# The beginning of a two-block transformer kernel, reordered: tokens and weights first, mem in the second head group, small rows through ScalarE's queue, angles on GpSimd

## Chip, cores and metric

The kernel runs on one core of a Trainium2 chip. The metric is the time of one launch on the device, in microseconds; lower is better.

## What is computed

256 tokens of width 1024 go through a first block of two layers and then a second block of two layers. All tensors are fp32. Each layer of the first block reads one large product of the tokens with `w_in` and splits it over three branches: a gated state-space branch (SSD, in both directions), differential attention with rotated queries and keys, and cross attention to 256 `mem` tokens.

```python
cos, sin = _rope_tables(positions)               # angle = position * inv_freq
for layer in range(2):
    proj = einsum('bsd,de->bse', x, w_in[layer])
    z, xbc, dt_raw, dq, dk, dv, dg, cq, cg, gl = split(proj)
    # SSD branch
    xbc = silu(conv5(xbc) + conv_b)              # 5 taps along the tokens
    dt = softplus(dt_raw + dt_bias);  a = -exp(a_log)
    y = scan(xs*dt[0], dt[0]*a[0], B, C) + flip(scan of the flipped) + d_skip*xs
    y_ssd = rmsnorm(y * silu(z))
    q, k = rope(dq, cos, sin), rope(dk, cos, sin)
    ...                                          # differential attention
    mem_kv = einsum('bmd,de->bme', mem, w_mem_kv[layer])
    ...                                          # cross attention, gates, output, layer norm
```

## The kernel before

**Products in three passes.** Weights come by DMA in units of 128 x 2048 fp32 (two transfers of 512 KB) into three raw buffers (`raw` slots 0 and 1, and `raw_third`, which lies in `scratch`). A unit is two weight tiles. `split(Q, p)` rounds tile p on ScalarE to a short mantissa (`w_hi`, L1082) and then VectorE stores the rest (`w_lo`, L1583). Four tiles are kept, so tile p+4 can be split only when TensorE has finished tile p. `x` and `mem` are split in the same way. TensorE's `proj` then runs 8 x 3 matmuls for each tile of 128 output columns (L583 to L585).

**Before the first product.** SyncE (SP) issues the identity, the positions, five constant columns, mem (two transfers, into `scratch`), x (two transfers), weight unit 0, the small rows (`early_params`, seven transfers), unit 1, then 16 transfers in `late_params` (the 1032 KB of constants, the step weights `w_dt` of both layers, `params_in` and the late rows). Unit 2 waits for `mem_ready`, because its buffer `raw_third` overlaps `mem_tok`. TensorE runs products with zeros (`idle_products`, L665) between transposing mem into four PSUM banks and x into four others (L673). VectorE works out the rotation angles (L1592 to L1608), ScalarE takes their sine and cosine.

**Head groups.** The SSD branch goes over four groups g of eight heads in each layer, each with tiles k = 0 to 15. For the six convolution tiles j = 0 to 5, ScalarE copies the PSUM bank to `conv_in`, applies the first tap, and splits weight tile j+4; VectorE adds the four other taps (`conv`, L1806), does its half of the split of tile j+4, and finishes the activation of tile j-1 (L1811). Tiles 6 to 9 are z, tiles 10 to 15 gates. In group 0 there is also the step size: `dt_tiles` (48 small matmuls, L732 to L734), `dt_exponent` and `dt_softplus` on VectorE ending in `a_tok` (L1792), the sums over tokens by `cumulate` (L743 to L750), and ScalarE's copies of these. Then, in every group, `spread_rows` (L792), the decays on ScalarE, `weigh` on VectorE (L1852) and `head_pair` on TensorE (L805).

**Order.** Each engine runs its own program in the order written, and the engines meet at semaphores. TensorE goes through group 0 of layer 0 as tile 0 (`first_tile`), transposes of rows, tiles 1 and 2, a wait for `tabs_in`, `dt_tiles`, tiles 3 to 8.

Of the kernel before, what the change touches and what calls it, by code (L numbers as in the profile page):

```python
# [7 lines left out]
F32 = mybir.dt.float32  # L8
# [7 lines left out]
P = 128  # L16
# [68 lines left out]
WARM_MEM, WARM_X, WARM_W = 4, 4, 8  # L85
# [75 lines left out]
def build(nc, a):  # L161
    ctx = ExitStack()
    with ctx:
# [107 lines left out]
        cut = Cut(SCRATCH - 2 * D)  # L271
        mem_tok = cut(2, D)

# [7 lines left out]
        mem_banks = (ps[5], ps[6], ps[0], ps[1])  # L281
# [55 lines left out]
        w_dt_in = sem("w_dt_in")  # L337
# [36 lines left out]
        def _(sp):  # L374
# [10 lines left out]
            load(pos_in, pos_i, spread(a["positions"][0]))  # L385
            const_cols(K_INV, 5, pos_in)
            for src, dst, s in ((a["mem"][0], mem_tok, mem_in), (a["x"][0], x_tok, x_in)):
# [4 lines left out]
            def early_params():  # L392
                load(rows_in, rows_a[0:PA_ROWS, :, :], a["conv_w"].rearrange("l k (t p) -> (k t) l p", p=P))
                for at, src in ((PB_CONVB, a["conv_b"]), (PB_NORM, a["ssd_norm_w"]), (PB_LNG, a["ln_g"]),
                                (PB_LNB, a["ln_b"]), (PB_DNW, a["diff_norm_w"])):
                    n = src.shape[1] // P
                    load(rows_in, rows_b[at:at + n, :, :], src.rearrange("l (t p) -> t l p", p=P))
                load(rows_in, rows_b[PB_GATE:PB_GATE + 24, :, :], a["gate_b"].rearrange("l b (t p) -> (b t) l p", p=P))

            def late_params():  # L400
                const_cols(P, K_INV - P, tabs_in)
                const_cols(K_SUB, P, tabs_in)
                for l in range(DEPTH):
                    load(w_dt_in, w_dt[:, l, :, :], a["w_in"][l].rearrange("(k p) c -> p k c", p=P)[:, :, DT0:DT0 + 64])
                    if l == 0:
                        for dst, src in ((neg_a, a["a_log"]), (dt_bias, a["dt_bias"])):
                            load(params_in, dst.rearrange("p l n -> p (l n)"), spread(src.rearrange("l d h -> (l d h)")))
                        load(params_in, skip_all.rearrange("p l n -> p (l n)"), spread(a["d_skip"].rearrange("l h -> (l h)")))
                        load(params_in, lam_in.rearrange("p l n -> p (l n)"), spread(a["diff_lam"].rearrange("l a b -> (l a b)")))
# [28 lines left out]
            for l in range(DEPTH):  # L438
                L = l * L1_Q
                for g in range(GROUPS):  # L440
                    Q = L + g * 4 + A_Q
                    cols(Q, 0, l, "w_in", X0 + g * 512)
                    if l == g == 0:
                        early_params()
                    cols(Q, 1, l, "w_in", X0 + 256 + g * 512)
                    if l == g == 0:
                        late_params()
                    if g == 0:
                        if l == 0:
                            sp.wait_ge(S["mem_ready"], 4)  # L450
                        else:
                            sp.wait_ge(S["merged_ready"], l * 4)
                    halves(Q, 2, l, "w_in", B0 + g * P, C0 + g * P)
# [67 lines left out]
        def _(pool):  # L521
# [8 lines left out]
            pool.memset(idle, 0.0).then_inc(S["idle_ready"], 1)  # L530
            pool.wait_ge(params_in, 16 * 4)
# [25 lines left out]
        def _(pe):  # L557
# [147 lines left out]
            def first_tile():  # L705
# [12 lines left out]
                pe.wait_ge(S["xT_ready"], 2)  # L718
                pe.wait_ge(tabs_in, 32)

            tri_le, tri_ge = mu[:, 0:P], ml[:, P:2 * P]
            for l in range(DEPTH):
                L, LH = l * L1_Q, l * L1_H + SETUP_H

                def dt_tiles():
                    pe.wait_ge(S["dt_lo_ready"], l + 1)
# [25 lines left out]
                for g in range(GROUPS):  # L752
                    Q, T, G = L + g * 4 + A_Q, LH + g * 8 + A_H, l * GROUPS + g
                    if g == 0:
# [4 lines left out]
                        dt_tiles()  # L759
                    for k in range(3 if g == 0 else 0, 9):  # L760
                        if l == g == 0 and k == 3:
                            pe.wait_ge(S["rows_free"], 1)
                        proj(Q, T, k, k, x1, own=ps[5] if g == 0 and k == 3 else None)
                        if l == g == 0 and k == 5:
# [14 lines left out]
                    if g == 0:  # L779
                        for k in range(9, 9 + 1):  # L780
                            proj(Q, T, k, k, x1)
                        cumulate()
# [294 lines left out]
        def _(act):  # L1077
# [60 lines left out]
            for b in range(4):  # L1138
                act.wait_ge(S["mem_turned"], b + 1)
                copy(mem_hi[:, 2 * b:2 * b + 2, :], pair(mem_banks[b])).then_inc(S["mem_hi_ready"], 1)  # L1140
            act.wait_ge(S["angles_ready"], 1)
            fn(sinT[:, :], red[:, 0, :], ACT.Sin, scale=const[:, K_SIGN:K_SIGN + 1])
            fn(cosT[:, :], red[:, 1, :], ACT.Sin).then_inc(S["rope_ready"], 1)
# [18 lines left out]
            act.wait_ge(tabs_in, 32)  # L1162

            def dt_weights(l):
                act.wait_ge(w_dt_in, 16 * DEPTH)
# [26 lines left out]
            dt_weights(0)  # L1192
            for l in range(DEPTH):
                L, LH = l * L1_Q, l * L1_H + SETUP_H
                turned_layers = l + 1
                for g in range(GROUPS):
# [9 lines left out]
                    zeros = view(const, K_CAUS2, 6, 2)  # L1206
                    copy(conv_in[:, :, 0:2], zeros)
                    copy(conv_in[:, :, 2 + SEQ:4 + SEQ], zeros)
                    for j in range(6):
# [7 lines left out]
                        split(Q, j + 4)  # L1217
# [1006 lines left out]
```

## Time and profile before

| | |
|---|---|
| median of 3 runs | 2443.31 us (2442.24 to 2443.97) |
| profiled execution | 2443.01 us, its span 2441.1 us |
| TensorE matmul | busy 2391.5 us (98%) |
| VectorE | busy 1713.4 us (70%) |
| ScalarE | busy 1339.5 us (55%) |
| GpSimd | busy 90.2 us (4%) |
| mean granted TensorE clock | 0.994 of full speed |

Times inside the profile count from the start of the span. The two clock levels of TensorE, 1.2 and 2.4 GHz, show as 0.5 and 1.0 in the column PEclk. A busy TensorE is not TensorE at its peak: the ends of matmuls are modelled, so starts are the better measure.

### The profile page before, as it was taken

The numbers are of one execution on the slowest core, as the hardware profiler recorded it, in microseconds if no ns is written. First come the engines' busy times: TensorE is split into PE (matmuls) and PEld (weight loads), VectorE is DVE, ScalarE is ACT, GpSimd is POOL, SyncE is SP. The second block draws the span as 40 slices with busy tenths as digits, with TensorE's granted clock in tenths as the row PEclk, the third lists the DMA queues.
The fourth block names the chain that finished last, engine by engine and source line by source line (L and its number), as shares of the span: only waits on it lengthen the run. The fifth ranks groups of instructions, "written<-read, shape, count | busy, mean of one in ns | idle before, by whom it ended". The sixth has DMA issues, their size and how long they took to land.

```text
span 2441.1 us, 48177 instructions
## 1 busy us (share of the span) xinstructions
PE 2391.5 (98%) x18842; PEld 2289.4 (94%) x18842; DVE 1713.4 (70%) x2517; ACT 1339.5 (55%) x2355; POOL 90.2 (4%) x101
## 2 busy tenths in 40 slices
PE   9999999999999999999999999999999999999998
PEld 8898999999899999999999997899999999789998
DVE  7788777777888867786766575676566657667665
ACT  6788655644678855563444445554444444555443
POOL 0000000000100000000100010010001001001000
PEclk9999999999999999999999999999999999999999
DMA  7454555455354455545455553345545544434553
GB/s 216 131 159 126 165 164 161 154 170 189 108 153 139 137 156 160 169 155 181 145 181 174 169 160 106 121 144 178 170 147 179 178 163 152 123 124 142 189 181 113
DMA packets 401046, 380.19 MB, mean 156 GB/s; under 512 B 28223, under 2 KB 397037, under 8 KB 400765
## 3 DMA queue, kind: packets, MB, share of 16 engines
q1 hardware_dynamic: 397821, 373.87, 48.0%
q10 hardware_dynamic: 3072, 4.20, 0.7%
q8 instruction: 106, 1.74, 0.3%
q14 instruction: 47, 0.39, 0.1%
HBM read 372.77 MB, written 1.05 MB: 153 GB/s over the span
## 4 chain that ended last, share of the span: by engine, by line
PE 79%; DVE 12%; ACT 3%; DVEq 3%; issue 1%; SPq 1%; DMA 1%; ACTq 0%
PE ps L583 22%; PE ps L585 21%; PE ps L584 21%; DVE scratch L1806 3%; DVE w_lo L1583 3%; DVEq L1805 2%; PE ps L805 2%; PE ps L836 1%; PE ps L837 1%; PE ps L838 1%; ACT scratch L1082 1%; ACT w_hi L1082 1%; PE ps L854 1%; PE ps L612 1%; PE ps L614 1%
## 5 line engine op out<-in xcount | busy, mean ns | idle before, releaser
L1583 DVE TENSOR_TENSOR w_lo<-raw,w_hi 128x1024 fp32r<-128x1024 f32 x664 | 812.0, 1229 | 423.2 <-ACT w_hi L1082 421.8
L583 PE MATMUL ps<-x_hi,w_hi 128*128 128x256 f32 (+1 forms) x3664 | 1056.4, 288 | 4.3 <-DVE w_lo L1583 1.6
L584 PE MATMUL ps<-x_lo,w_hi 128*128 128x256 f32 (+1 forms) x3664 | 1042.6, 285 | 0.0
L585 PE MATMUL ps<-x_hi,w_lo 128*128 128x256 f32 (+1 forms) x3664 | 1039.8, 284 | 0.0
L1082 ACT ACTIVATE w_hi<-raw 128x1024 fp32r<-128x1024 f32 x664 | 697.7, 1056 | 447.5 <-PE ps L585 370.6
L583 PEld LDWEIGHTS ps<-x_hi,w_hi 128*128 128x128 f32 x3664 | 690.8, 189 | 30.8 <-issue 25.3
L584 PEld LDWEIGHTS ps<-x_lo,w_hi 128*128 128x128 f32 x3664 | 692.2, 189 | 2.0
L585 PEld LDWEIGHTS ps<-x_hi,w_lo 128*128 128x128 f32 x3664 | 693.6, 189 | 0.0
L583 PE MATMUL ps<-big_r,w_hi 128*128 128x272 f32 (+1 forms) x832 | 238.9, 287 | 0.0
L585 PE MATMUL ps<-big_r,w_lo 128*128 128x272 f32 (+1 forms) x832 | 238.2, 286 | 0.0
L1082 ACT ACTIVATE scratch<-ps 128x256 f32<-128x256 f32 (+9 forms) x328 | 122.3, 384 | 154.9 <-PE ps L838 63.8
L584 PE MATMUL ps<-gates_r,w_hi 128*128 128x272 f32 (+1 forms) x704 | 201.3, 286 | 0.0
L584 PE MATMUL ps<-big_r,w_hi 128*128 128x256 f32 (+1 forms) x640 | 181.3, 283 | 0.0
L1079 ACT ACTIVATE scratch<-ps 128x256 f32<-128x256 f32 (+2 forms) x168 | 66.6, 399 | 168.8 <-PE ps L585 153.8
L585 PEld LDWEIGHTS ps<-big_r,w_lo 128*128 128x128 f32 x832 | 156.6, 188 | 0.0
L583 PEld LDWEIGHTS ps<-big_r,w_hi 128*128 128x128 f32 x832 | 156.3, 188 | 0.2
L583 PE MATMUL ps<-scratch_r,w_hi 128*128 128x256 f32 x512 | 144.2, 282 | 2.6 <-DVE scratch L1995 2.6
L585 PE MATMUL ps<-scratch_r,w_lo 128*128 128x256 f32 x512 | 144.7, 283 | 0.0
L584 PEld LDWEIGHTS ps<-gates_r,w_hi 128*128 128x128 f32 x704 | 132.5, 188 | 0.1
L584 PEld LDWEIGHTS ps<-big_r,w_hi 128*128 128x128 f32 x640 | 120.1, 188 | 0.1
L527 POOL TENSOR_TENSOR xT<-xT,norm_bias 128x272 f32<-128x272 f32 (+1 forms) x56 | 52.0, 961 | 1688.4 <-DVE x_lo L1713 1688.4
L1806 DVE SCALAR_TENSOR_TENSOR scratch<-scratch,pa_all 128x256 f32<-128x256 f32 x192 | 93.5, 487 | 24.8 <-ACT scratch L1079 12.7
(302 smaller groups left out, 3063.1 us busy)
## 6 DMA issues: line engine op xcount, KB each, us to landing
raw<-in_w_in SPq DMA_DIRECT2D x184, 512.0 KB, 4.7
raw<-in_ffn_w_up SPq DMA_DIRECT2D x176, 512.0 KB, 4.3
raw<-in_ffn_w_down SPq DMA_DIRECT2D x64, 512.0 KB, 4.2
raw<-in_mix_w_in SPq DMA_DIRECT2D x64, 512.0 KB, 4.6
scratch<-in_w_in SPq DMA_DIRECT2D x40, 512.0 KB, 4.8
raw<-in_w_mem_kv SPq DMA_DIRECT2D x32, 512.0 KB, 4.8
raw<-in_w_br_ssd SPq DMA_DIRECT2D x32, 512.0 KB, 3.8
raw<-in_ffn_w_down SPq DMA_DIRECT2D x32, 384.0 KB, 3.3
```

The costliest lines, as they stand in the source:

```text
L527: m = pool.tensor_tensor(x, x, norm_bias[:, o:o + 1].to_broadcast([P, n]), ALU.add)
L583: mm(out, wh, xh, start=first, stop=False)
L584: mm(out, wh, xl, start=False, stop=False)
L585: return mm(out, wl, xh, start=False, stop=last)
L612: mm(out, w_hi[:, o, j, :], x[0][:, j, :], start=(j == 0), stop=False)
L614: mm(out, w_lo[:, o, j, :], x[0][:, j, :], start=False, stop=False)
L805: m = mm(b[e * 64:(e + 1) * 64, q], x_dt[:, 2 * d + t, j * 64:(j + 1) * 64], decay[:, j % 4, w], start=(n == 0), stop=(n == 3), skip_group ...
L1079: return act.activation(out, in_, f, **kw)
L1082: return act.activation(out, in_, ACT.Copy, scale=scale)
L1583: tt(w_lo[:, p % PARTS, :, :], raw_at(slot_of(Q, p))[:, :, (p % 2) * P:(p % 2 + 1) * P], wh_f[:, p % PARTS, :, :], ALU.subtract).then_inc( ...
L1805: v.drain()
L1806: m = stt(c, conv_in[:, j, n:n + SEQ], tap(n), c, ALU.mult, ALU.add)
```

## The change

- **SP's order:** identity, x, unit 0, unit 1, then `step_params` (positions, five constant columns, `w_dt` of layer 0, the four `params_in` transfers), unit 2 without a wait, then `late_params` (constants and late rows), units 3 and 4. After unit 4 SP waits for `rope_ready` and issues mem and `w_dt` of layer 1. mem_tok now lies in `gates`, over the angle buffers.
- **Small rows:** the seven transfers of `early_params` are issued by ScalarE as its first work.
- **Angles:** the work is moved from VectorE to GpSimd. A fused multiply-add becomes a `tensor_scalar` and a `tensor_tensor`: 15 instructions, most of them behind a drain.
- **Sine and cosine:** on ScalarE after `dt_weights(0)`, ahead of the first convolution tile, instead of ahead of x.
- **mem:** transposed, copied and split in group 1 of layer 0: `turn_mem(b)` stands before tile k = 2b on TensorE, `mem_copy(b)` on ScalarE behind the split of tile 2b+4 (the last one behind z tile 0), `mem_rest(b)` on VectorE behind the split of tile 2b+4 (the last one ahead of `conv_silu(5)`). One PSUM bank, ps[5], serves all four; from b = 1 on TensorE waits until `mem_rest(b-1)` is done.
- **dt_tiles** of layer 0 come after tile 4 instead of after tile 2; `dt_exponent` and its Exp two convolution tiles later. The waits for the constants move to just before their first use.

```diff
-WARM_MEM, WARM_X, WARM_W = 4, 4, 8
+WARM_X, WARM_W = 8, 8
...
+        mem_tok = view(gates, 4096, 2, D)
...
+            tokens_in(a["x"][0], x_tok, x_in)
...
+            def step_params():
+                load(pos_in, pos_i, spread(a["positions"][0]))
+                const_cols(K_INV, 5, pos_in)
+                step_weights(0)
...
                     cols(Q, 1, l, "w_in", X0 + 256 + g * 512)
                     if l == g == 0:
+                        step_params()
+                    if g == 0 and l:
+                        sp.wait_ge(S["merged_ready"], l * 4)
+                    halves(Q, 2, l, "w_in", B0 + g * P, C0 + g * P)
+                    if l == g == 0:
                         late_params()
-                    if g == 0:
-                        if l == 0:
-                            sp.wait_ge(S["mem_ready"], 4)
...
                     cols(Q, 4, l, "w_in", Z0 + 256 + g * 512)
+                    if l == g == 0:
+                        sp.wait_ge(S["rope_ready"], 1)
+                        tokens_in(a["mem"][0], mem_tok, mem_in)
+                        step_weights(1)
...
+            pool.wait_ge(pos_in, 32)
+            pool.tensor_copy(red[:, 2, :], pos_i)
+            pool.drain()
+            pts(an, red[:, 2, :], const[:, K_INV:K_INV + 1], None, ALU.mult)
...
+            for c in (C1, C2, C3):
+                pool.drain()
+                pts(red[:, 1, :], red[:, 3, :], -c, None, ALU.mult)
+                pool.drain()
+                ptt(an, red[:, 1, :], an, ALU.add)
...
+            pts(red[:, 1, :], red[:, 1, :], PI_DOWN, -PI_DOWN, ALU.min, ALU.max).then_inc(S["angles_ready"], 1)
             pool.wait_ge(params_in, 16 * 4)
...
             pe.wait_ge(S["idle_ready"], 1)
-            idle_products(ps[7], WARM_MEM)
+            idle_products(ps[7], WARM_X)
             pe.wait_ge(ident_in, 16)
-            turn_tokens(mem_tok, mem_banks, mem_in, "mem_turned")
-            idle_products(ps[7], WARM_X)
             turn_tokens(x_tok, x_banks, x_in, "x_turned")
-            pe.wait_ge(S["mem_ready"], 1)
             idle_products(ps[5], WARM_W)
-            pe.wait_ge(S["mem_ready"], 4)
+
+            def turn_mem(b):
+                pe.wait_ge(mem_in[b // 2], 16)
+                if b:
+                    pe.wait_ge(S["mem_ready"], b)
+                for f in range(2 * b, 2 * b + 2):
+                    for t in range(2):
+                        m = pe.transpose(ps[5][:, (f % 2) * SEQ + t * P:(f % 2) * SEQ + (t + 1) * P], mem_tok[:, t, f * P:(f + 1) * P], ident)
+                m.then_inc(S["mem_turned"], 1)
...
+                        if l == 0 and g == 1 and k in (0, 2, 4, 6):
+                            turn_mem(k // 2)
                         proj(Q, T, k, k, x1, own=ps[5] if g == 0 and k == 3 else None)
+                        if l == g == 0 and k == 4:
+                            dt_tiles()
...
             x_copy(0)
             x_copy(1)
             dt_weights(0)
+            rope_tables()
+            act.wait_ge(S["idle_ready"], 1)
...
                         split(Q, j + 4)
+                        if l == 0 and g == 1 and j in (0, 2, 4):
+                            mem_copy(j // 2)
...
                         split(Q, j + 4)
+                        if l == 0 and g == 1 and j in (0, 2, 4):
+                            mem_rest(j // 2)
                         if j:
                             conv_silu(j - 1)
-                        if g == 0 and j == 1:
+                        if g == 0 and j == (1 if l else 3):
                             dt_exponent()
```

## Rows read from the trace of the kernel before

**Rows 1.** Timeline, SyncE's queue: start us, us, queue line, transfer, count.
```profile
2.13 0.94 SPq L390 DMA_DIRECT2D scratch<-in_mem  x2
```

**Rows 2.** Timeline, first 32 us: start us, us, engine, instruction [idle before, releaser].
```profile
7.54 3.17 PE L673 MATMUL ps<-const,scratch 128*128 128x128 f32 x16 [2.65 <-DMA scratch<-in_mem]
...
18.06 0.36 PE L710 MATMUL ps<-x_hi,w_hi 128*128 128x256 f32 x1
...
18.08 2.01 ACT L1082 ACTIVATE w_hi<-raw 128x1024 fp32r<-128x1024 f32 x2 [0.66 <-DMA raw<-in_w_in]
...
25.15 0.30 ACT L1082 ACTIVATE scratch<-const 128x12 f32<-128x12 f32 x2
...
30.25 1.06 ACT L1082 ACTIVATE w_hi<-scratch 128x1024 fp32r<-128x1024 f32 x1 [3.84 <-DMA scratch<-in_w_in]
```

**Rows 3.** Windows from the start: busy of PE, PEld, DVE, ACT, POOL; PEclk, DMA share, GB/s.
```profile
0.00:9.00 9.00, 5.24 (x17) 3.76 (x18) 2.85 (x9) 1.96 (x3) 0.52 (x5) 0.95 0.69 206
...
0.00:18.00 18.00, 14.24 (x64) 11.75 (x64) 9.94 (x21) 9.72 (x14) 0.52 (x5) 0.91 0.90 278
```

**Rows 4.** Timeline, VectorE, group 0: conv(0), w_lo of tile 4.
```profile
26.72 2.16 DVE L1806 SCALAR_TENSOR_TENSOR scratch<-scratch,pa_all 128x256 f32<-128x256 f32 x4
31.34 1.22 DVE L1583 TENSOR_TENSOR w_lo<-scratch,w_hi 128x1024 fp32r<-128x1024 f32 x1 [2.46 <-ACT w_hi L1082]
```

**Rows 5.** Timeline, TensorE, group 0: start of dt_tiles, of tile 3, of cumulate.
```profile
27.07 0.19 PE L732 MATMUL ps<-w_dt_hi,x_hi 128*128 128x64 f32 x1
...
32.61 0.56 PE L583 MATMUL ps<-x_hi,w_hi 128*128 128x256 f32 x1
...
57.98 0.30 PE L743 MATMUL ps<-a_tok,const 128*128 128x32 f32 x1 [1.23 <-DVE a_tok L1792]
```

**Rows 6.** Timeline, GpSimd: a fill, four copies with drains, two adds of one shape.
```profile
0.74 0.31 POOL L530 MEMSET gates<- 128x256 f32 x1 [0.29 <-POOLq L2212]
23.66 1.15 POOL L535 COPY skip<-skip_all 64x16 f32<-64x16 f32 x4 [22.61 <-DMA gates<-in_diff_lam]
...
90.40 1.47 POOL L549 TENSOR_TENSOR y_sum<-y_sum,y_sq 128x256 f32<-128x256 f32 x1 [8.50 <-ACT y_sq L1079]
95.03 0.74 POOL L549 TENSOR_TENSOR y_sum<-y_sum,y_sq 128x256 f32<-128x256 f32 x1 [3.17 <-ACT y_sq L1079]
```

**Rows 7.** Timeline, ScalarE: sine and its cosine before; a table load ahead of a wait.
```profile
12.66 0.51 ACT L1079 ACTIVATE sinT<-gates,const 128x256 f32<-128x256 f32 x1
...
319.39 1.28 ACT L1079 ACT_TABLE_LOAD   x1
324.69 0.63 ACT L1079 ACTIVATE scratch<-scratch 128x512 f32<-128x512 f32 x1 [4.02 <-DVE scratch L1968]
```

**Rows 8.** Windows, TensorE alone: us, busy (count), PEclk, DMA share, GB/s.
```profile
8.50:12.00 3.50, 3.50 (x15) 0.56 1.07 374
...
32.00:35.30 3.30, 3.30 (x17) 0.51 0.91 290
...
623.00:633.20 10.20, 10.20 (x50) 0.52 0.39 117
```

**Rows 9.** Timeline, TensorE, group 1: starts of tiles 1, 2, 8, and head pair 0.
```profile
95.03 0.28 PE L583 MATMUL ps<-x_hi,w_hi 128*128 128x256 f32 x1
...
97.88 0.28 PE L583 MATMUL ps<-x_hi,w_hi 128*128 128x256 f32 x1
...
115.34 0.36 PE L583 MATMUL ps<-x_hi,w_hi 128*128 128x256 f32 x1 [0.18 <-DVE w_lo L1583]
...
128.31 1.52 PE L805 MATMUL ps<-big,scratch 128*64 128x256 f32 x16 [1.11 <-DVE big L1852]
```

**Rows 10.** Timeline: ScalarE's copy of tile 0 in group 1, VectorE's split behind conv(0), mem's split.
```profile
96.61 0.36 ACT L1082 ACTIVATE scratch<-ps 128x256 f32<-128x256 f32 x1
...
100.14 1.22 DVE L1583 TENSOR_TENSOR w_lo<-raw,w_hi 128x1024 fp32r<-128x1024 f32 x1
...
9.94 2.48 DVE L1616 TENSOR_TENSOR mem_lo<-ps,mem_hi 128x512 fp32r<-128x512 f32 x4
```

More of the change, by code:

```diff
@@ L336, in build @@
         late_rows_in = sem("late_rows_in")
-        w_dt_in = sem("w_dt_in")
+        w_dt_in = [sem(f"w_dt_in{l}") for l in range(DEPTH)]
         rot_in = [sem("q_rotated_in"), sem("k_rotated_in")]
@@ L384, in _, with tokens_in @@
             const_cols(K_ID, P, ident_in)
-            load(pos_in, pos_i, spread(a["positions"][0]))
-            const_cols(K_INV, 5, pos_in)
-            for src, dst, s in ((a["mem"][0], mem_tok, mem_in), (a["x"][0], x_tok, x_in)):
+            def tokens_in(src, dst, s):
                 for h in range(2):
@@ L390, in _, with step_weights @@
                     sp.dma_start(dst[:, :, c], src.rearrange("(t p) d -> p t d", p=P)[:, :, c]).then_inc(s[h], 16)
[L392 to L398, printed above, removed]
+            tokens_in(a["x"][0], x_tok, x_in)
+            def step_weights(l):
+                load(w_dt_in[l], w_dt[:, l, :, :], a["w_in"][l].rearrange("(k p) c -> p k c", p=P)[:, :, DT0:DT0 + 64])
+            def step_params():
+                load(pos_in, pos_i, spread(a["positions"][0]))
+                const_cols(K_INV, 5, pos_in)
+                step_weights(0)
+                for dst, src in ((neg_a, a["a_log"]), (dt_bias, a["dt_bias"])):
+                    load(params_in, dst.rearrange("p l n -> p (l n)"), spread(src.rearrange("l d h -> (l d h)")))
+                load(params_in, skip_all.rearrange("p l n -> p (l n)"), spread(a["d_skip"].rearrange("l h -> (l h)")))
+                load(params_in, lam_in.rearrange("p l n -> p (l n)"), spread(a["diff_lam"].rearrange("l a b -> (l a b)")))
             def late_params():
@@ L781, in _ @@
                             proj(Q, T, k, k, x1)
+                        pe.wait_ge(tabs_in, 32)
                         cumulate()
@@ L1136, in pair, with load, mem_copy, rope_tables @@
                 return bank[:, :].rearrange("p (f s) -> p f s", f=2)
-            for b in range(4):
-                act.wait_ge(S["mem_turned"], b + 1)
[L1140 to L1143, printed above, removed]
+            def load(s, dst, src):
+                act.dma_start(dst, src).then_inc(s, 16)
+            load(rows_in, rows_a[0:PA_ROWS, :, :], a["conv_w"].rearrange("l k (t p) -> (k t) l p", p=P))
+            for at, src in ((PB_CONVB, a["conv_b"]), (PB_NORM, a["ssd_norm_w"]), (PB_LNG, a["ln_g"]),
+                            (PB_LNB, a["ln_b"]), (PB_DNW, a["diff_norm_w"])):
+                n = src.shape[1] // P
+                load(rows_in, rows_b[at:at + n, :, :], src.rearrange("l (t p) -> t l p", p=P))
+            load(rows_in, rows_b[PB_GATE:PB_GATE + 24, :, :], a["gate_b"].rearrange("l b (t p) -> (b t) l p", p=P))
+            def mem_copy(b):
+                act.wait_ge(S["mem_turned"], b + 1)
+                copy(mem_hi[:, 2 * b:2 * b + 2, :], pair(ps[5])).then_inc(S["mem_hi_ready"], 1)
+            def rope_tables():
+                act.wait_ge(S["angles_ready"], 1)
+                fn(sinT[:, :], red[:, 0, :], ACT.Sin, scale=const[:, K_SIGN:K_SIGN + 1])
+                fn(cosT[:, :], red[:, 1, :], ACT.Sin).then_inc(S["rope_ready"], 1)
             def x_first(b):
@@ L1203, in conv_tanh @@
                         fn(xbc_t[:, j % 2, :], xbc[:, j, :], ACT.Tanh).then_inc(S["conv_tanh"], 1)
-                    zeros = view(const, K_CAUS2, 6, 2)
+                    zeros = view(gates, 0, 6, 2) if l == g == 0 else view(const, K_CAUS2, 6, 2)
                     copy(conv_in[:, :, 0:2], zeros)
@@ L1226, in _ @@
                                 late_copies()
-                        if g == 0 and j == 2:
+                        if g == 0 and j == (2 if l else 4):
                             act.wait_ge(S["dt_pre"], l + 1)
@@ L1240, in _ @@
                     z_tile(0)
+                    if l == 0 and g == 1:
+                        mem_copy(3)
                     conv_tanh(5)
@@ L1589, in _, with mem_rest @@
             v.sem_inc(lo_ready, LO_CREDIT)
[L1590 to L1608 removed]
             def pair(bank):
                 return bank[:, :].rearrange("p (f s) -> p f s", f=2)
[L1613 removed]
+            def mem_rest(b):
                 v.wait_ge(S["mem_hi_ready"], b + 1)
                 t = slice(2 * b, 2 * b + 2)
[L1616 removed]
+                tt(mem_lo[:, t, :], pair(ps[5]), mem_hi[:, t, :].bitcast(F32), ALU.subtract).then_inc(S["mem_ready"], 1)
             def x_rest(b):
```

63 lines of the change are left out of this document (21 added, 42 removed).

## Prediction

> **What bounds the kernel now.** I read the busy shares first. TensorE is busy 98% of the span and at full clock nearly all the time, so over the whole launch there are only some 50 us that an edit of the order could win back, and the edit touches the first 130 us alone. I then read the timeline of the start. The first product begins at 18.06; before it mem is waited for, turned and split, and only then x [rows 2]. The chain that ended last runs through the first 31 us as SP issues, one transfer (unit 2), and ScalarE's split of tile 4: that split begins at 30.25 after 3.84 of waiting for the transfer [rows 2]. VectorE has finished conv(0) by then and starts the rest of tile 4 at 31.34 [rows 4]. From there VectorE has hardly a gap until `a_tok`, and TensorE waits 1.23 for it and starts the sums at 57.98 [rows 5]. So an earlier product at the start is worth nothing by itself: what counts is when tile 4 is split, and what engine is the last one at 57.98.
>
> In group 1 TensorE is the bound, but only just. It is delayed 0.18 before tile 8 and 1.11 before head pair 0 by VectorE [rows 9]. VectorE needs about 3.55 us for each convolution tile (2.15 for four taps, 1.15 for the split, 0.35 for the activation; rows 4 and 10 show the first two), TensorE 2.85 [rows 9]. TensorE gets through the nine tiles because it enters them with four tiles split ahead.
>
> **The start.** x is asked for at the place where mem was or earlier (mem at 2.13 [rows 1]), about 0.9 us sooner. Mem's first half ended TensorE's wait at 7.54 [rows 2], so x's should by about 6.4. ScalarE's seven issues fit before that, in a stretch where it only waited. The first product can then begin some 4 to 5 us earlier than 18.06, near 13.3. Tiles 0 to 3 and the rows take 11.8 us, so TensorE is through with tile 3 near 25.1 and then has nothing until tile 4 is split. I count no gain for this.
>
> Unit 1 before was waited for until 18.08, with 4.6 MB asked for up to it (identity, positions, mem, x, two units, rows). Between 9 and 18 us the queue moved (278 x 18 - 206 x 9) / 9 = 350 GB/s [rows 3]. Up to the positions and constant columns there are now 3.6 MB, 1.0 MB less or 2.9 us, and the stream starts 0.9 sooner: they land near 14.3. Unit 2 has 1.8 MB more before its end: near 19.5. It is no longer late. The mem transfers come behind unit 4 and the sines, and have 40 us before their use: nothing.
>
> **The angles now set tile 4.** ScalarE does the sines before the first convolution tile and in order, so the conv, the split of tile 4 and all that follows stand behind `angles_ready`. GpSimd runs 15 instructions: 11 with one input, 4 with two. The trace has no one-input arithmetic there; its bounds are the fill of the same shape, 0.31, and the add, 0.74 by itself and 1.47 beside a VectorE split [rows 6]. A drain adds 0.1: four tiny copies of which each takes 0.19 spread over 1.15. I take 0.4 for the one-input form, nearer the fill, since it too has one stream to move. Sum: 11 x 0.52 + 4 x 0.86 = 9.2, and 1.0 for meeting the last splits of tiles 2 and 3. Angles are ready at 14.3 + 10.2 = 24.5. With 0.31 and no meeting it is 22.5; with 0.92 for one input (twice my 0.4, and more) and 1.47 for the four adds, 32.
>
> The GPSIMD Engine Reference of the Trainium skill (Engine selection, Specifications) sends elementwise work to VectorE, calls two-input work about twice as slow on GpSimd and one-input work roughly line-rate, and says that two-input VectorE instructions contend with it. The trace agrees on the last: the same add took 0.74 and 1.47. By that page one-input work would be nearer the lower bound, and the sum would come out nearer 23.
>
> The sine's table load costs 1.28 but was made ahead of a wait elsewhere (load at 319.39, instruction at 324.69 [rows 7]); here it is hidden in the same way. Sine and cosine cost 0.9 [rows 7]: 25.4. From ScalarE's zeros at 25.15 to the end of conv(0) at 28.88 took 3.7 [rows 2, 4]; I take 3.5, without the wait in it for VectorE's other work. So conv(0) ends at 28.9 and VectorE splits tile 4 from 28.9 to 30.1, 2.4 us sooner than before.
>
> **The last engine of group 0.** VectorE needs 57.98 - 31.34 = 26.6 from there to `a_tok`: 55.5. TensorE before ran from tile 3 at 32.61 to 56.75 (57.98 less the wait of 1.23 [rows 5]), 24.1, of which 1.35 is the half clock until 35.3 [rows 8]. At full clock, less tile 3 (2.85) and with dt_tiles (27.07 to 32.61, 5.2 at full clock [rows 5]), it needs 22.8 - 2.85 + 5.2 = 25.2 from tile 4 on. dt_tiles used to fill the wait for unit 2; now they come behind it. So TensorE idles some 4.8 us, and is then the last engine: 30.1 + 25.2 = 55.3, plus the clock. After an idle stretch of 2.65 [rows 2] the granted clock fell to 0.56 (8.5 to 12), and behind dt_tiles to 0.51 (32.0 to 35.3) and in layer 1 for 10.2 us [rows 8]. One such stretch costs 1.7; here there are both causes, so 1.7 to 3.4. The sums begin between 57.0 and 58.7, against 57.98. I take -0.3 for group 0.
>
> **Mem in group 1.** TensorE now does 16 transposes, VectorE four splits of 0.62 [rows 10], ScalarE four copies of 0.6. Before, they lay ahead of the first product. The larger cost is the wait in `turn_mem(b)`. It asks that VectorE be through conv(2b-2) and the split of tile 2b+2, which TensorE needs only two tiles later. All in times of before, with copy, tap and conv 3.5 (96.61 to 100.14 [rows 10]):
> - Tile 0 starts 0.5 late, for its own transposes; tile 1 ends at 97.88 + 0.5 = 98.4. VectorE ends the split of tile 4 at 101.3 and mem's at 101.95. TensorE waits 3.5, transposes 0.5, and starts tile 2 at 102.5 instead of 97.88.
> - Tile 2 ends at 105.35; conv(2) and its split follow, 3.5 + 1.2, then mem's: 110.65. Tile 3 ended at 108.2. Wait 2.4; tile 4 at 111.1.
> - Tile 4 ends at 113.95; 117.5, 119.3. Tile 5 ended at 116.8. Wait 2.5; tile 6 at 119.8, tile 8 at 125.5 instead of 115.34.
>
> That is 10.2 late at tile 8. TensorE cannot give it back: it has no other gap than the 1.11 before head pair 0, which goes, because VectorE is now ahead. Net +9.1. An idle stretch of 3.5 is longer than the 2.65 after which the clock fell, so I add one half-clock stretch, +1.7. Behind that, queued on TensorE, the spread rows, head pairs and gate tiles of group 1 all shift; group 2 starts late by the same amount.
>
> The sum is 2443.0 (the profiled execution's own time, 0.3 under the median) - 0.3 + 9.1 + 1.7 = 2453.5, and as a median 2453.5 too within its error.
>
> **Rivals.**
> - *Fast angles (not slower by more than the bound).* If the positions land by 11 and the one-input form costs 0.31, the angles are ready by 19.5, unit 2 lands at the same time, and tile 4 is ready before TensorE ends tile 3 at 25.1. Then there is no idle stretch: 25.1 + 25.2 + 1.7 = 52.0, 6.0 sooner. With +9.1 in group 1 and no fall of the clock there, 2446. It decides once angles are ready before 21. For it: the fill's 0.31 and the short queue. Against it: 3.6 MB ahead of the positions at 350 GB/s.
> - *Slow angles.* At 32, tile 4 comes 7.5 later: 2461. For it: 1.47 beside splits; against it: the splits end by 17.
> - *The clock.* The 10.2 us of half clock in layer 1 [rows 8] cost 5.1; if that stretch is cut to 3.4 us by the shift in time, 3.4 come back: 2450. If both mem waits and dt_tiles bring a stretch more, 2456.
> - *Mem is covered after all (faster).* If TensorE's waits were as short as VectorE's added work, group 1 would cost 2.5; with the fast angles that gives 2443.0 - 6.0 + 2.5 = 2439.5, and with the shorter stretch of layer 1, 2436. Against it: the wait is written before tile 2, and VectorE cannot be done before 101.9.
>
> **Chances.** My forecast with its clock variants (2449 to 2457) 0.55, fast angles 0.22, slow angles 0.13, mem covered 0.10. The range reaches from between fast angles and no change to slow angles, 2444 to 2461. Within 0.2% is within 4.9 us, about what a measurement of this kernel can tell from no change. Slower: 0.55 + 0.13; within: 0.22 and a part of the last, 0.25; faster: 0.07.
>
> **What would show it.** In the profile after: the first product near 13.3; VectorE free of angles; 15 GpSimd instructions ending near 24.5 and the sine right behind; unit 2 not waited for; TensorE idle some 5 us before tile 4, then dt_tiles; `cumulate` near 57.7. In group 1, three waits of TensorE for VectorE's mem split before tiles 2, 4 and 6, of 3.5, 2.4 and 2.5, and no wait before head pair 0. The prediction is wrong if the angles come before 21 or after 28, if the waits in group 1 are under 1 us each, or if the stretches of half clock move by more than one.

## The result, and the profile after

The changed kernel takes 2464.75 us (median of 4, 2459.12 to 2465.14) against 2443.64 before: ratio 1.0083, interval 1.0071 to 1.0095. It is slower by 21 us, outside the range given and twice the 10 us forecast. The profiled execution took 2465.14 us, its span is 2463.3 us, 22.2 longer than before.

The tiles of TensorE show where the time went. The first two rows are the changed kernel's: first product and tile 4. The others are the starts of group 1 and group 2 (timeline, TensorE: start us, us).

```profile
14.31 0.36 PE L735 MATMUL ps<-x_hi,w_hi 128*128 128x256 f32 x1 [0.82 <-issue]
...
38.70 0.58 PE L603 MATMUL ps<-x_hi,w_hi 128*128 128x256 f32 x1 [12.37 <-ACT scratch L1111]
...
104.13 0.36 PE L603 MATMUL ps<-x_hi,w_hi 128*128 128x256 f32 x1
...
174.20 0.39 PE L603 MATMUL ps<-x_hi,w_hi 128*128 128x256 f32 x1
```

The same point, the start of group 2, in the kernel before (timeline, TensorE):

```profile
149.85 0.39 PE L583 MATMUL ps<-x_hi,w_hi 128*128 128x256 f32 x1
```

The first product is 3.7 us sooner than at 18.06 [rows 2], and that bought nothing. Tile 4 started at 36.81 before; now it is at 38.70, behind a gap of 12.37. Group 1 began at 92.08 before and now at 104.13: 12.05 us were lost in group 0 (0.4 of it is mem's first transposes, which stand just ahead of this mark). Group 2 is 24.35 late, so group 1 lost 12.3 more. After that 2.15 us come back, most of it in the half clock of layer 1 (6.8 us of it instead of the 10.2 of [rows 8]). "Half clock" here and below is a stretch in which the column PEclk shows 0.5.

**Group 0.** GpSimd in the changed kernel (timeline: start us, us, what ended the idle time):

```profile
15.68 0.40 POOL L530 CAST gates<-gates 128x256 f32<-128x256 int32 x1 [14.63 <-DMA const<-constants]
16.33 2.80 POOL L532 TENSOR_SCALAR gates<-gates,const 128x256 f32<-128x256 f32 x1 [0.25 <-issue]
19.29 0.41 POOL L534 TENSOR_SCALAR gates<-gates 128x256 f32<-128x256 f32 x1 [0.15 <-issue]
19.84 0.86 POOL L536 TENSOR_SCALAR gates<-gates 128x256 f32<-128x256 f32 x1 [0.15 <-issue]
20.86 0.97 POOL L539 TENSOR_SCALAR gates<-gates 128x256 f32<-128x256 f32 x1 [0.15 <-issue]
21.98 0.73 POOL L541 TENSOR_TENSOR gates<-gates 128x256 f32<-128x256 f32 x1
...
30.24 0.40 POOL L550 TENSOR_SCALAR gates<-gates 128x256 f32<-128x256 f32 x1 [0.16 <-issue]
```

GpSimd can start on the positions at 15.68, and its chain takes 15.0 us. The two-input adds cost 0.73, as the row of before had it [rows 6]. The one-input `tensor_scalar` instructions are of two kinds, 0.41 and 0.85 or more, and the first took 2.80. ScalarE waits for the end of it (timeline, ScalarE, changed kernel):

```profile
20.05 1.28 ACT L1108 ACT_TABLE_LOAD   x1
30.68 0.51 ACT L1108 ACTIVATE sinT<-gates,const 128x256 f32<-128x256 f32 x1 [9.34 <-POOL gates L550]
...
37.12 0.29 ACT L1108 ACTIVATE neg_a<-neg_a 128x128 f32<-128x128 f32 x1
37.44 0.71 ACT L1111 ACTIVATE head_sel<-const 64x32 fp32r<-64x32 f32 x3
38.17 0.20 ACT L1108 ACTIVATE stats<-stats 128x4 f32<-128x4 f32 x1
38.28 0.37 ACT L1111 ACTIVATE scratch<-ps 128x256 f32<-128x256 f32 x1
```

and VectorE has two splits beside the 2.80 of GpSimd, tile 4's split and, later, a wait (timeline, VectorE, changed kernel):

```profile
16.05 2.36 DVE L1630 TENSOR_TENSOR w_lo<-raw,w_hi 128x1024 fp32r<-128x1024 f32 x2 [0.71 <-ACT w_hi L1111]
...
34.76 1.22 DVE L1630 TENSOR_TENSOR w_lo<-scratch,w_hi 128x1024 fp32r<-128x1024 f32 x1
...
51.20 0.22 DVE L1787 TENSOR_TENSOR big<-ps,dt_bias_b 128x64 f32<-128x64 f32 x1 [3.90 <-PE ps L758]
```

The table load is indeed hidden in the wait. Tile 4 is split from 34.76 to 35.98, and yet TensorE starts it 2.7 us later: it waits for a count that ScalarE raises with its copy of tile 2 (38.28), which stands behind `small_params` (37.12 to 38.28). The count is stricter than the data: tile 4 goes into ps[0], whose tile 0 ScalarE copied at 31.60, and tile 2 lies in ps[6], but the copies of tiles 0 and 2 raise one semaphore, and `bank` asks for both:

```python
def bank(T, k):
    pe.wait_ge(gf[k % 2], T + k // 2 + 1)
...
bank = {2: ps[6], 3: ps[5]}.get(j, ps[j % 2]) if g == 0 else ps[j % 2]
copy(conv_in[:, j, 2:2 + SEQ], bank[:, 0:SEQ]).then_inc(gf[j % 2], 1)
```

Then VectorE waits 3.90 for `dt_tiles`. Part of TensorE's work here runs at half clock, as its windows of the changed kernel show (us, busy (count), PEclk, DMA share, GB/s):

```profile
31.00:44.60 13.60, 5.90 (x28) 0.50 0.60 191
48.00:54.80 6.80, 6.80 (x34) 0.50 0.43 146
75.40:82.20 6.80, 6.27 (x27) 0.50 0.00 0
```

The first stretch begins inside the gap, so only 5.9 us of it are work. The step-size sums begin at 69.69 instead of 57.98, and TensorE has no wait ahead of them, so it is the last engine, as forecast (timeline, TensorE, changed kernel):

```profile
69.69 1.42 PE L767 MATMUL ps<-a_tok,const 128*128 128x32 f32 x12
```

Between tile 3 and the sums the kernel before had one stretch, from 32.0 to 35.3 [rows 8]; now there are the first two. The third lies behind the start of the sums, where the kernel before had 6.8 us as well.

**Group 1.** TensorE's waits in the changed kernel over the whole span (who waited for whom: us in total, times, longest):

```profile
PE ps L603 <- ACT scratch L1111: 12.4, 1, 12.4
PE ps L709 <- DVE mem_lo L1643: 8.3, 3, 3.3
...
PE ps L834 <- DVE big L1882: 6.1, 6, 1.1
```

and two of the waits with mem's transposes and the tile behind the first (timeline, TensorE):

```profile
113.38 1.09 PE L709 MATMUL ps<-const,gates 128*128 128x128 f32 x4 [3.30 <-DVE mem_lo L1643]
114.12 0.56 PE L603 MATMUL ps<-x_hi,w_hi 128*128 128x256 f32 x1
...
133.74 1.09 PE L709 MATMUL ps<-const,gates 128*128 128x128 f32 x4 [2.62 <-DVE mem_lo L1643]
```

The third wait, of 2.33, ends at 123.36. Each comes with 3.4 us of half clock, which begins inside the wait (windows, changed kernel):

```profile
112.90:116.30 3.40, 2.92 (x14) 0.50 0.00 0
```

The two others begin near 123.2 and 133.5. The wait before head pair 0 [rows 9] is gone.

### The profile page after: what moved, and what is told of

Its sections match the earlier page's. It is cut to its first block, busy times and chain, and to the rows that moved or that the text cites. A ratio compares the mean times of both kernels' runs of the same rounds, so it can differ in the third digit from the quotient of the medians.

```text
span 2463.3 us, 48167 instructions
## 1 busy us (share of the span) xinstructions
PE 2397.1 (97%) x18842; PEld 2296.0 (93%) x18842; DVE 1711.4 (69%) x2506; ACT 1339.4 (54%) x2355; POOL 103.0 (4%) x116
## 4 chain that ended last, share of the span: by engine, by line
PE 80%; DVE 11%; ACT 4%; DVEq 2%; issue 2%; DMA 1%; POOLq 1%; ACTq 0%; SPq 0%; POOL 0%
PE ps L603 22%; PE ps L605 22%; PE ps L604 22%; DVE scratch L1831 3%; DVE w_lo L1630 2%; PE ps L834 2%; DVEq L1830 1%; PE ps L865 1%; PE ps L866 1%; PE ps L867 1%; ACT scratch L1111 1%; ACT w_hi L1111 1%; DMA raw<-in_ffn_w_up 1%; PE ps L883 1%; DVE xT L1732 1%
```

## The experiments

All are edits of the changed kernel unless a line says otherwise. Marks are from the profiled execution, one for each kernel, in us from its start. The launches are medians and were taken on different chips; the ratio is to the kernel before on the same chip, so launches are best compared by it.

| kernel | sine starts | tile 4 | group 1 | group 2 | launch | ratio (interval) |
|---|---|---|---|---|---|---|
| before | 12.66 | 36.81 | 92.08 | 149.85 | | 1 |
| changed | 30.68 | 38.70 | 104.13 | 174.20 | 2464.75 | 1.0083 (1.0071 to 1.0095) |
| a1 angles on VectorE | 24.94 | 32.97 | 98.20 | 170.21 | 2461.74 | 1.0070 (1.0054 to 1.0087) |
| a2 four banks | 30.00 | 38.02 | 103.48 | 162.88 | 2454.40 | 1.0043 (1.0027 to 1.0060) |
| a3 dt_tiles early | 30.78 | 38.81 | 98.13 | 168.12 | 2458.19 | 1.0062 (1.0045 to 1.0079) |
| a4 two-operation forms | 28.12 | 36.15 | 99.11 | 169.64 | 2462.41 | 1.0080 (1.0063 to 1.0096) |
| b1 = a1 + a2 + a3 | 25.69 | 34.24 | 91.03 | 150.78 | 2443.26 | 1.0002 (0.9993 to 1.0012) |
| b2 positions first | 21.16 | 29.21 | 93.57 | 163.64 | 2455.26 | 1.0048 (1.0032 to 1.0063) |
| b3 all mended | 20.91 | 34.24 | 87.22 | 146.99 | 2439.85 | 0.9984 (0.9975 to 0.9993) |
| b4 gap filled | 30.40 | 38.43 | 99.95 | 170.45 | 2466.02 | 1.0097 (1.0082 to 1.0113) |
| c1 copy freed | 29.73 | 36.59 | 95.97 | 166.53 | 2464.27 | 1.0087 (1.0071 to 1.0102) |
| c2 halves, both layers | 20.87 | 30.96 | 84.55 | 144.32 | 2439.91 | 0.9985 (0.9976 to 0.9994) |
| c3 filled and banks | 31.03 | 39.06 | 100.44 | 159.82 | 2454.67 | 1.0043 (1.0028 to 1.0059) |
| d1 halves, layer 0 | 21.47 | 31.56 | 85.14 | 144.92 | 2437.43 | 0.9978 (0.9969 to 0.9987) |

The intervals of a1, a3, a4, b4 and c1 overlap that of the changed kernel: for these the marks show where time moved, and a gain of the launch is not shown by itself. The marks also hold what half clock that one execution had. The clearest case is c1: its group 1 starts 8.2 sooner than in the changed kernel although tile 4 is only 2.1 sooner, since this execution had 10.2 us of half clock ahead of group 1 instead of 27.2.

### Angles back on VectorE

```diff
-            pool.wait_ge(pos_in, 32)
...
             dt_weights(0)
             lam_products()
+            v.wait_ge(pos_in, 32)
+            v.tensor_copy(red[:, 2, :], pos_i)
...
```

> The changed kernel with the twelve angle instructions back on VectorE, behind its work on the step weights and lambda. In the changed kernel GpSimd had the angles ready at 30.64 us and ScalarE had waited 9.34 us for them. If the GpSimd chain is what sets tile 4 (theory), VectorE starts at about 21.6, needs 4.4 us as before, sine follows at 26.0, and everything behind it moves up by 4.6 us; TensorE's gap of 12.4 us before tile 4 shrinks to about 7.8, and with less half clock the launch gains 4.6 to 8 us. If the place of the sines in ScalarE's order or its copy of tile 2 is what counts and not the engine (rival), the launch moves by less than 1.5 us.

The sine starts 5.7 us sooner (4.6 expected), tile 4 also 5.7. The gap is 7.98 and the half clock that begins in it 10.2 us instead of 13.6. Some 1.4 of the 5.7 is the first product, which came sooner in this execution. Group 2 is only 4.0 sooner, with 3.4 us more of half clock in group 1 (6.8, 3.4 and 3.4), and the launch 3.0, under the 4.6 expected and within the intervals. GpSimd's chain is on the path to tile 4; what it costs the launch this run alone does not show.

### Four banks for mem

```diff
                 pe.wait_ge(mem_in[b // 2], 16)
-                if b:
-                    pe.wait_ge(S["mem_ready"], b)
...
-                copy(mem_hi[:, 2 * b:2 * b + 2, :], pair(ps[5]))
+                copy(mem_hi[:, 2 * b:2 * b + 2, :], pair(mem_banks[b]))
```

`mem_banks` holds ps[5], ps[7], ps[2] and ps[3], and the split of the low part reads the same bank.

> The changed kernel with four PSUM banks for mem (ps[5], ps[7], ps[2], ps[3]) instead of one, so that TensorE no longer waits for VectorE's split of the last pair; mem's work and places stay. If the single bank's handshake is the cost in group 1 (theory), the three waits of 3.30, 2.33 and 2.62 us go, TensorE then keeps VectorE's pace and reaches tile 8 about 7 us sooner, the three half-clock stretches (3.4 us each, 1.7 us of loss each) go too: 8 to 13 us in all. If mem's own work on VectorE and ScalarE is the cost and the waits only show it (rival), the time comes back before tile 8 or head pair 0 and the launch gains under 3 us.

From group 1 to group 2 it takes 59.4 us, against 70.1 in the changed kernel and 57.8 before. The three waits and the three stretches of half clock are gone; two small waits for VectorE are back in their old places (0.94 where it was 0.16 before, and 1.10 before head pair 0). The launch gains 10.4, and its interval is clear of the changed kernel's. Mem's own work in group 1 costs 1.6, besides the 0.4 of transposes ahead of the mark; the single bank's handshake costs 10.7. Nearly all of the 10.7 can be named: 8.25 of waits and 4.1 of clock (each of tiles 2, 4 and 6 takes 3.9 to 4.0 us instead of 2.9, and the transposes ahead of it 0.74 instead of 0.41), less the two small waits that come back.

### dt_tiles early

```diff
                             first_three(Q, T, x1, l * KT, SEQ)
-                            dt_tiles()
+                        dt_tiles()
...
-                        if l == g == 0 and k == 4:
-                            dt_tiles()
```

> The changed kernel with dt_tiles back behind tile 2, so that they fill the gap of 12.4 us before tile 4. If their place cost time (theory), TensorE loses their 7 us at half clock behind tile 4, VectorE's waits for them (0.46 and 3.90 us) go, and the launch gains 7 to 12 us. If group 0 is set by VectorE's chain from the split of tile 4 to a_tok anyway (rival), it gains only VectorE's waits, 4 us or less.

Tile 4 stays where it was (38.81, gap 4.04) and tile 5 starts at 43.09 instead of 50.98. Group 1 is 6.0 sooner and the launch 6.6. TensorE now waits 1.40 for `a_tok`: VectorE's chain is the next bound, so the gain is under the 7 us expected but above the rival's 4.

### Two-operation forms on GpSimd

```diff
+            pts(an, idle, 1.0, 0.0, ALU.mult, ALU.add)
             pool.wait_ge(pos_in, 32)
...
-                pts(red[:, 1, :], red[:, 3, :], -c, None, ALU.mult)
+                pts(red[:, 1, :], red[:, 3, :], -c, 0.0, ALU.mult, ALU.add)
```

> The changed kernel with the five tensor_scalar instructions of GpSimd that have one operation (0.85 to 0.97 us each) given a second one that changes nothing (times 1 or plus 0), and a tensor_scalar on zeros while GpSimd waits for the positions. If the one-operation form is the slow one (theory), each falls to the 0.41 of the two-operation forms, 2.3 us together. If the 2.80 us of the first tensor_scalar were the first use of the form, it falls to below 1; if they are its per-partition scalar, it stays at 2.8. The angles come 2.3 to 4.3 us sooner and the launch gains that, up to 2 us more with the clock. Rival: the times go with the operations and values and not with the form: the five stay at 0.85 or more, no gain.

GpSimd in this kernel (timeline):

```profile
1.30 0.41 POOL L530 TENSOR_SCALAR gates<-gates 128x256 f32<-128x256 f32 x1 [0.25 <-issue]
15.11 0.40 POOL L532 CAST gates<-gates 128x256 f32<-128x256 int32 x1 [13.40 <-DMA const<-constants]
15.68 2.88 POOL L534 TENSOR_SCALAR gates<-gates,const 128x256 f32<-128x256 f32 x1 [0.17 <-issue]
...
21.67 0.41 POOL L541 TENSOR_SCALAR gates<-gates 128x256 f32<-128x256 f32 x1 [0.16 <-issue]
...
25.03 1.08 POOL L546 TENSOR_SCALAR gates<-gates 128x256 f32<-128x256 f32 x1
```

A second operation that does nothing halves the instruction: 0.41 instead of 0.85. It is the form. Of the five edited ones only the one at 19.84, which ran beside VectorE's split of the step weights, stayed at 0.80. A `tensor_scalar` at 1.30 did not help the first of the chain (2.88), so the first use of the instruction is not its cost; that one took two constants, while the first of the chain takes one scalar for each partition, and the kernel with the positions first (below) settles what is left. The chain is 13.0 instead of 15.0. The launch is 2.3 lower, within the scatter of these launches.

### The three undone together

> The changed kernel with all three of the single edits at once: angles on VectorE, four PSUM banks for mem, dt_tiles behind tile 2. Alone they moved the start of group 2 (104 us of TensorE tiles later) by 4.0, 11.3 and 6.1 us. If the three costs are separate (theory), their sum of 21 us comes back and the launch is at 2443 to 2445, no different from the kernel before. If they overlap, since angles and dt_tiles both live off the same gap (rival), 3 to 6 us less come back: 2447 to 2450.

2443.26, no different from before. The three together account for the whole 21 us, and they add up (4.0, 11.3 and 6.1 at group 2 alone; 23.4 together). Against four banks alone (1.0043) the other two bring a further 10 to 11 us of the launch, clear of the intervals, so what a1 and a3 leave open for one edit is shown for both. Group 2 starts 0.9 behind the kernel before.

### Positions first

```diff
+            load(pos_in, pos_i, spread(a["positions"][0]))
+            const_cols(K_INV, 5, pos_in)
             tokens_in(a["x"][0], x_tok, x_in)
```

> The changed kernel with the positions and the five constant columns asked for ahead of x, as before the change; the angles stay on GpSimd. If it is the sum of a late request and a slow chain that sets tile 4 (theory), GpSimd starts near 5.6 instead of 15.7, needs 15 us and is done at 20.6 instead of 30.6; the sines are then hardly waited for, tile 4 starts near 28.5 instead of 38.7, TensorE's gap is under 3 us, and with less half clock the launch gains 10 to 14 us. If the DMA queue and unit 2 are the next thing late (rival), tile 4 moves up by 5 us or less.

GpSimd in this kernel (timeline):

```profile
5.47 0.40 POOL L530 CAST gates<-gates 128x256 f32<-128x256 int32 x1 [4.41 <-DMA const<-constants]
6.11 0.93 POOL L532 TENSOR_SCALAR gates<-gates,const 128x256 f32<-128x256 f32 x1 [0.25 <-issue]
...
11.66 0.73 POOL L541 TENSOR_TENSOR gates<-gates 128x256 f32<-128x256 f32 x1
...
16.02 1.95 POOL L544 TENSOR_SCALAR gates<-gates 128x256 f32<-128x256 f32 x1
...
20.14 0.70 POOL L550 TENSOR_SCALAR gates<-gates 128x256 f32<-128x256 f32 x1 [0.16 <-issue]
```

VectorE beside it (timeline):

```profile
10.10 2.48 DVE L1648 TENSOR_TENSOR x_lo<-ps,x_hi 128x512 fp32r<-128x512 f32 x4 [10.10 <-ACT x_hi L1111]
12.69 5.68 DVE L1630 TENSOR_TENSOR w_lo<-raw,w_hi 128x1024 fp32r<-128x1024 f32 x4
```

The chain ends at 20.84, ScalarE does not wait for it, tile 4 starts at 29.21 with a gap of 3.04, and the launch gains 9.5, a little under the 10 expected and clear of the intervals. Unit 2 is not the next thing late: the gap left is again the wait for the copy of tile 2 (28.79), for tile 4 is split by 26.47. The rows also show what the 2.80 was: the same instruction takes 0.93 at 6.11, while VectorE is idle, and the one at 16.02 takes 1.95 beside VectorE's splits of weights where it took 1.09 in the changed kernel, with VectorE idle. VectorE pays too: its four splits take 5.68, against 2.36 for two in the changed kernel. The splits of x, which read one of their inputs from PSUM, do not slow GpSimd: the add at 11.66 takes 0.73 beside them. The Trainium skill's GPSIMD Engine Reference (Specifications) names this contention, with VectorE instructions that have two inputs in SBUF; both runs agree.

### All mended

Positions first, angles at VectorE's start as before the change, dt_tiles early, four banks. x and units 0 to 2 early, small rows by ScalarE, mem in group 1 and the late sines are kept.

> The changed kernel's order (x and both first units early, small rows through ScalarE's queue, mem in group 1) with its three costs mended: positions asked for first and the angles on VectorE at the start as before, sines where the change has them, dt_tiles behind tile 2, four PSUM banks for mem. Theory: unit 2 is no longer late, ScalarE reaches the first convolution tile near 22.3, TensorE passes from tile 3 to tile 4 without a gap, and the step-size sums begin near 52 instead of 57.98, 5.7 us sooner than in the kernel before; mem in group 1 costs 1.6 us (59.4 us from group 1 to group 2 with four banks, 57.8 before). Sum: 2443.3 - 4.1 = 2439. Rival: what was hidden behind unit 2 before is now late itself (sines, ScalarE's copies), and the launch stays within 2 us of the kernel before.

2439.85, ratio 0.9984 (0.9975 to 0.9993): faster than before by 3.5 us (2443.33 beside it), near the forecast of 4.1. Group 1 starts 4.9 sooner, and the sums at 54.0, not at the 52 expected: half clock of 6.8 us stays, from 27.3 within `dt_tiles`. So the new order, with these costs mended, gains a little. VectorE's angles from 5.6 us on cost nothing that shows, since it waits for x then anyway.

### The gap filled, alone and with four banks

```diff
+                        if l == g == 0 and k == 4:
+                            pe.wait_ge(S["xT_ready"], 2)
+                            idle_products(ps[2], 27)
```

> The changed kernel with 27 products of zeros into ps[2] ahead of tile 4, to fill TensorE's gap of 12.4 us; nothing else is changed. If the half clock behind the gap (13.7 us and, behind dt_tiles, 6.8 us more) is a cost of its own (theory), TensorE stays at full clock up to dt_tiles, tile 4 and dt_tiles take 8.1 instead of 12.3 us, and the launch gains 3.5 to 6 us. If dt_tiles bring the half clock by themselves (rival), it gains under 2 us.

> The changed kernel with four banks for mem (2454.4 us) and also 27 products of zeros in the gap before tile 4. The filling alone brought the start of group 2 forward by 3.75 us but left the launch where it was. If the half clock behind the gap is a real cost and the rest was the scatter of the launch (theory), this one is 3 to 5 us under the kernel with four banks, near 2450.5. If filling the gap costs again later what it gives (rival), it stays within 1.5 us of 2454.4.

TensorE in the first of these (windows: us, busy (count), PEclk, DMA share, GB/s):

```profile
26.00:38.40 12.40, 11.76 (x55) 1.00 0.81 253
38.40:46.60 8.20, 8.17 (x68) 0.94 0.44 131
```

Tile 4 now runs at full clock and tile 5 starts at 47.60, 3.4 us sooner. Tile 4 and `dt_tiles` take 9.2 us, not the 8.1 expected, since 6.8 us of half clock between 44 and 53 stay: `dt_tiles` bring these without the gap, as the rival said. Group 2 is 3.75 sooner (3.06 with four banks). The launches did not move: 2466.02 and 2454.67 (four banks alone 2454.40). With four banks layer 1 had 10.2 and 6.8 us of half clock against 6.8 in all without the filling. In the other the time went back bit by bit: TensorE is 3.8 ahead of the changed kernel near 154 us, 3.0 near 685, 1.7 near 1450, 1.0 near 2107 and 0.4 at the end, although this execution had 33 us of half clock against 52. So the half clock that begins in the gap is a real loss at its place, and no gain of the launch was measured from removing it. Why is open.

### ScalarE's copy freed

```diff
-                            if j == 1:
+                            if j == 4:
                                 small_params()
```

> The changed kernel with small_params on ScalarE behind convolution tile 4 instead of tile 1, so that its four small pieces (1.2 us from 37.12 to 38.28 in the changed kernel) no longer stand ahead of the copy of tile 2, for which TensorE waits before tile 4. If that copy and not the split of tile 4 (done at 35.98) is what lets TensorE go (theory), tile 4 starts 1.2 us sooner, at 37.5, and the next tiles with it; if the split is (rival), tile 4 does not move. The launch's own change, 1 to 2 us, is near what the timing can tell.

Tile 4 starts 2.1 sooner, and 0.95 of that is the earlier sine; the rest, 1.15, is the 1.2 of `small_params`. It is the copy that TensorE waits for. What a count without tile 2 would give, up to the 2.7 us between split and start, no run tried. The profiled execution had a single stretch of 10.2 us of half clock before group 1, and took 2458.12; the three others took 2464.2 to 2464.9. No gain in the launch is shown.

### dt_tiles in halves

Two edits of the mended kernel (b3). The first cuts `dt_tiles` in both layers, and also moves `dt_exponent` and its Exp in layer 1 two convolution tiles later; the second cuts them in layer 0 alone. The lines are the first's, against the changed kernel.

```diff
-                        dt_tiles()
+                        dt_tile(0)
...
+                        if g == 0 and k == 3:
+                            dt_tile(1)
```

> The mended kernel (2439.85 us) with dt_tiles cut in its two token halves, the second half behind tile 3, in both layers; dt_exponent and its Exp in layer 1 where the change put them in layer 0. In the mended kernel dt_tiles were followed by 6.8 us of half clock in layer 0 (27.3 to 34.1) and 6.8 plus 3.4 in layer 1, a loss of up to 8.5 us. If 48 matmuls of 64 columns in a row bring the half clock (theory), 24 in a row with a dense tile between bring less: one or both stretches go, a gain of 3 to 8 us. If any stretch with small matmuls of that number in the neighbourhood brings it (rival), nothing changes but the order: within 1 us.

> The mended kernel with dt_tiles cut in two halves in layer 0 alone; layer 1 keeps them in one piece. With halves in both layers the half clock of layer 0 was gone (group 2 began 2.7 us sooner) but layer 1 showed 13.7 us of it against 10.2 in the mended kernel. If cutting is what brought more of it in layer 1 (theory), this kernel keeps both gains, 2437.2 us. If the half clock of layer 1 goes by chance with where in time its dt_tiles fall (rival), it is 2437 to 2443 and within its interval of 2439.9.

TensorE in the mended kernel, and then in the one with halves in layer 0 (windows):

```profile
27.30:34.10 6.80, 6.80 (x36) 0.56 1.10 348
```

```profile
19.90:31.50 11.60, 11.60 (x104) 1.00 1.07 338
619.20:626.00 6.80, 6.80 (x35) 0.54 0.12 26
653.30:656.70 3.40, 3.40 (x19) 0.57 0.00 0
```

With tile 3 between the halves the clock stays full there in layer 0, and group 2 starts 2.7 us (both layers) and 2.1 us (layer 0 alone) sooner. In layer 1 the halves did not help: 13.7 us of half clock were there, and the launch was 2439.91, no gain. With one piece in layer 1 it is 6.8 plus 3.4 as in the mended kernel, and 2437.43, ratio 0.9978 (0.9969 to 0.9987), the lowest median here. The forecast was 2437.2. Its interval overlaps the mended kernel's (0.9975 to 0.9993), and the rival allowed 2437 to 2443, so neither a gain over the mended kernel nor the theory is shown. One profile of each does not settle whether the halves, the moved Exp or chance made layer 1 worse.

## Why the prediction was wrong

The direction and the two places, group 0 and group 1, were right; the size was half. Three steps failed: the price of GpSimd's one-input instructions, the split taken as the last wait of tile 4, and the number of half-clock stretches. Two of the prediction's own signs of being wrong came: the angles after 28, and more than one stretch of half clock more.

**The start, right.** First product forecast near 13.3, was 14.31; no gain from it. Unit 2 was not waited for. Sine directly behind the angles, table load hidden.

**Positions, 1.4 us off.** Forecast 14.3, came at 15.68. SP began to issue the positions at 5.70 and the constant columns only at 8.82; which part of the 1.4 that is, no run separates.

**The price of the one-input form, the mis-sized term.** I took 0.4 for all eleven because the fill of the same shape took 0.31. Of those with one operation five cost 0.85 to 0.97, and the first 2.80 beside two splits of VectorE; the ones with two cost 0.40 to 0.41, but 1.09 with a comparison. The chain measured 15.0 against 10.2, 4.8 us: 2.4 for the first, 2.4 for the five, 0.7 for the comparison and some 0.4 for the pauses between, less the 1.0 I had put on the meeting with VectorE, although the row of the add already showed a doubling [rows 6]. The slow-angles rival (32) was near what came (30.64), with a chance of 0.13, and in part by luck: it had all four adds slowed to 1.47, and they took 0.73.

**"Tile 4 is split" as the release of tile 4, wrong.** The step took the split for the last wait. TensorE also waits for a count that ScalarE raises with its copy of tile 2, behind `small_params`: 2.7 us more, and c1 moved it. Before the change the same copy at 36.01 stood just ahead of tile 4 at 36.81, and I did not ask why.

**The clock, under-counted.** I allowed 1.7 to 3.4 us in group 0 and 1.7 in group 1. In group 0, up to the sums, TensorE worked 5.9 and 6.8 us at half clock. By its starts tile 4 took 5.3 us where a tile at full clock takes 2.85, `dt_tiles` 7.0 where 5.2 was counted, and tile 5 4.6: 6.0 us lost. In group 1 there were three stretches of 3.4 instead of one, 4.1 lost. One stretch of 3.4 cost less than the 1.7 I took: a step of three products takes 0.64 at half clock and 0.355 at full, 1.8 times and not twice, and a stretch that begins in a wait is not all work. A longer gap before tile 4 went with a longer stretch: 12.37 and 13.6 us, 10.85 and 10.2, 10.21 and 10.2, 7.98 and 10.2, 4.04 and 3.4, 3.04 and 3.4 (changed kernel, c1, a4, a1, a3, b2).

**Sum of group 0.** Angles 1.4 + 4.8 late, the count 2.7, the clock 3.5 more than the 2.5 in the sum, less 0.4 for terms taken too large: 12.0, which is 69.69 - 57.98 less the -0.3 forecast.

**The handshake, right.** Waits forecast 3.5, 2.4 and 2.5, measured 3.30, 2.33 and 2.62; the wait before head pair 0 went. Tile 8 was 13.9 late within the group (forecast 10.2 and one stretch, 11.9), and the group lost 12.3 against 10.8: 2.4 more of clock, 0.9 less of the rest. The mem-covered rival fell with a2: what its 2.5 us describe is a kernel with four banks (1.6).

## What to carry to other kernels

Before work is moved to an idle engine, look at which queue will wait for its last result, and at every wait of the instruction that you take as released: here the tile waited for a split and for a count of copies, ran at half clock when it came, and only the split was counted. A semaphore that counts copies of several banks can hold a tile back although its own bank is free. A buffer that two engines hand back and forth ties a fast engine to a slow one's order, and here each of the three waits, of 2.3 to 3.3 us, also brought 3.4 us of half clock; three more banks, free at that time, took 10 us away. An early first product is worth only what the last engine of the stage makes of it.

## What the runs showed of the hardware

- On GpSimd a `tensor_scalar` of 128x256 fp32 with one operation took 0.85 us and with two 0.41, also when the second does nothing (a4); with a greater-than and a product it took 1.08.
- GpSimd's instruction of 0.93 us (b2, VectorE idle) took 2.80 and 2.88 (changed kernel, a4) next to two splits by VectorE with both inputs in SBUF; next to splits that read PSUM an add kept its 0.73.
- Half clock came with waits of TensorE as short as 2.33 us, and once, with no wait, within the 48 small matmuls of `dt_tiles` and behind them (6.8 us in b3).
- Of the four launches of the changed kernel one took 2459.12 with a mean granted clock of 0.993 and three 2464.4 to 2465.1 with 0.990. The difference of 0.003 over 2463 us is 15 us of half clock, some 7 us lost by this estimate: stretches come in some executions and not in others, and changes of 2 to 4 us in this kernel drown in that with four launches. The clock is not all of it: b4 took 2464.67 with 0.994.
